# Splitting the results of two attentions, and the first weights of their output projections, inside the attentions on GpSimd

## The chip, the cores and the metric

The kernel runs on one core of a Trainium2 chip. The metric is the device time of one execution in microseconds (us), as the median of several runs. The engines are TensorE (PE, and PEld for its weight loads), VectorE (DVE), ScalarE (ACT), GpSimd (POOL) and SyncE (SP, which issues the DMAs here).

## What is computed

The reference is three transformer layers on 512 latent tokens and 256 context tokens of width 1024. The first layer (a state-space mixer and a convolutional MLP) is not touched. The change lies behind the mixers of the second and third layer:

```python
# layer 2: y = [mlstm_out(ha, oa) (512 wide), window attention (512 wide)] @ w_out, for latent and context tokens
def mlstm_out(h, oa):
    h = rms_norm(h.transpose(0, 2, 1, 3), a_norm_g.reshape(A_HEADS, A_HEAD_DIM))
    return (h.reshape(...) * jax.nn.sigmoid(oa)).astype(oa.dtype)
ob_l = banded_window_attention(qb_l, kb_l, vb_l, kb_c, vb_c, sink)   # 8 heads of 64; context tokens: gqa_attend
y_lat = jnp.concatenate([mlstm_out(ha_l, oa_l), ob_l], axis=-1) @ w_out
# layer 3: y = attention(8 heads of 128, 512 queries on 768 keys) @ w_out, for latent tokens alone
y_lat = gqa_attend(q_blocks, k_all, v_all) @ w_out
# both: x = x + gate * y, and then the MLP
```

## The kernel before

Activations are kept transposed, as tiles of 128 features by tokens: `xT` (the residual stream) and `hT` are eight tiles of 768 tokens (512 latent, 256 context). Weights come as slabs of 1024 by 256 through a ring of four slots (`ring`), which SP fills.

A product of fp32 accuracy is made of three fp32r products. Each operand is split into a high part (rounded to fp32r, `_hi`) and a low part (the operand minus its high part, `_lo`), and PE multiplies hi by hi, hi by lo and lo by hi. The slab is split in two halves, m = 0 and 1, of 128 columns: ScalarE writes `w_hi` (L1232, 128x1024), GpSimd writes `w_lo` (L1237).

The program is a chain of blocks (`nc.Block`), with all engines meeting at a block's end. The blocks that matter here:

- `band_attention` (layer 2): 24 pairs p = (two heads, query block of 128 tokens), six query blocks for each of four pairs of heads. Blocks 0 to 3 are latent and 4 and 5 context, and the keys are 256 to 640 wide. For each pair PE makes the scores (L2714), DVE adds the mask and takes the maximum (`top`, L2773), ScalarE the exponential (L2811), DVE divides each of the two heads by its sum (`norm`, L2785, a TENSOR_SCALAR from SBUF to SBUF), PE transposes (L2726), ScalarE and DVE copy the transposes to SBUF (L2819 and L2793), PE multiplies by the values (L2740) and ScalarE copies the result to `hT` (`give`, L2825). PE runs the scores two pairs ahead. DVE's order is top(p+1), norm(p), the copy of p-1. GpSimd builds the masks, multiplies four tiles of `hT` by the gates (`side`, L2695, 128x768 each), and then has nothing to do.
- `attention` (layer 3): 32 jobs j = (head, block of 128 queries), all 768 keys wide, with the same steps: scores L2540, maximum L2584 (reads PSUM), exponential L2620, `norm` L2602 (TENSOR_SCALAR 128x768), transposes L2551, copy L2628 on ScalarE, values L2562, `give` L2635. GpSimd has no work in it.
- `output_projection`, once behind each (`ab_out` over 768 tokens, `c_out` over 512). It runs `split_stage` with `Halves` as what comes first: ScalarE makes the first slab's two high parts, GpSimd and DVE one low part each, then ScalarE writes the high parts of all of `hT` tile by tile (L662) and DVE the low parts (L667). PE follows tile by tile. For this first slab PE takes the two halves of the weights in turn at each tile, so that both halves are in use until the slab's end:

```python
def unit_order(n_r, first):
    return [(m, r) for r in range(n_r) for m in range(2)] if first else [(m, r) for m in range(2) for r in range(n_r)]
```

In the later slabs PE finishes half 0 before it takes half 1. The high and low part of a half of the next slab are written over those of the same half of the slab before, so ScalarE waits until PE is through with that half.

## Time and profile before

| | before |
|---|---|
| median of 3 runs | 2615.78 us (2614.35 to 2617.09) |
| the profiled execution, its time | 2614.36 us |
| the profiled execution, its span | 2612.6 us |
| mean granted TensorE clock | 0.954 |
| PE busy | 2381.1 us, 91% |
| PEld busy | 1929.9 us, 74% |
| DVE busy | 1231.2 us, 47% |
| ACT busy | 805.5 us, 31% |
| POOL busy | 1003.8 us, 38% |

The time is 1.8 us more than the span, which goes from the first to the last instruction. A share is busy time over the whole span. PE is the busiest by far, but it does not work through: inside an attention each engine waits for another, and between blocks PE waits for what it is to multiply. The second layer's attention lies at 1148 to 1266 us of the span and the third's at about 2068 to 2172 us.

### The profile page before, as it was taken

To read this page: it belongs to the slowest core of one execution; us is meant where nothing else is said; L and a number is where in the kernel's file an instruction comes from. 1 tells how busy PE (TensorE), PEld (TensorE's weight loads), DVE (VectorE), ACT (ScalarE), POOL (GpSimd) and SP (SyncE) were. 2 spreads that over 40 slices of the span, in tenths; PEclk is the share of its full clock that TensorE was granted. 3 is DMA by queue.
4 is the path that set the end of the run, shared out by engine and by line. 5 is a ranking of instruction groups with operands and counts; after the bars stand their busy time and mean duration, and the time that the engine had idled before them with its cause. 6 is when DMAs were issued, how large, how long until landed. Compare 5 with 4: busy or idle time off the path is not lost. (4 is left out here: it accounts for less than half of the span.)

```text
span 2612.6 us, 34942 instructions
## 1 busy us (share of the span) xinstructions
PE 2381.1 (91%) x14323; PEld 1929.9 (74%) x14323; DVE 1231.2 (47%) x1956; ACT 805.5 (31%) x1325; POOL 1003.8 (38%) x606
## 2 busy tenths in 40 slices
PE   6987688999997989967789999999989998899998
PEld 5866466777775779855668888888867687688887
DVE  4417627756555660567436242332427752423432
ACT  4232334333335412335332111111134363322221
POOL 3326234655553322320136343443434002555553
PEclk8998898999997999979899999999989999899999
DMA  8570213444441111100113233333311101233221
GB/s 266 161 226 1 75 49 113 157 153 154 149 145 58 40 48 59 33 1 1 33 49 97 81 113 114 114 127 100 113 41 65 33 1 49 65 97 97 96 97 49
DMA packets 224700, 229.94 MB, mean 88 GB/s; under 512 B 7375, under 2 KB 221219, under 8 KB 224547
## 3 DMA queue, kind: packets, MB, share of 16 engines
q1 hardware_dynamic: 224211, 227.66, 27.1%
q8 instruction: 113, 1.85, 0.3%
q14 instruction: 40, 0.33, 0.0%
q10 hardware_dynamic: 336, 0.11, 0.0%
HBM read 225.65 MB, written 2.10 MB: 87 GB/s over the span
## 5 line engine op out<-in xcount | busy, mean ns | idle before, releaser
L1237 POOL TENSOR_TENSOR w_lo<-ring,w_hi 128x1024 fp32r<-128x1024 f32 x128 | 311.5, 2434 | 431.5 <-ACT w_hi L1232 431.5
L1232 ACT ACTIVATE w_hi<-ring 128x1024 fp32r<-128x1024 f32 x128 | 135.6, 1059 | 738.4 <-PE ps L1297 701.9
L2039 DVE SCALAR_TENSOR_TENSOR xT<-ps,mods,xT 128x512 f32<-128x512 f32 (+1 forms) x160 | 108.3, 683 | 533.0 <-PE ps L1297 474.0
L1295 PE MATMUL ps<-hidden_hi,w_hi 128*128 128x512 f32 (+1 forms) x768 | 273.9, 357 | 5.4 <-POOL hidden_lo L2393 5.4
L1296 PE MATMUL ps<-hidden_lo,w_hi 128*128 128x512 f32 (+1 forms) x768 | 272.1, 354 | 0.0
L1297 PE MATMUL ps<-hidden_hi,w_lo 128*128 128x512 f32 (+1 forms) x768 | 271.6, 354 | 0.0
L2316 DVE SCALAR_TENSOR_TENSOR ffn_sums<-ps,cols,ffn_sums 128x441 f32<-128x441 f32 (+2 forms) x352 | 215.0, 687 | 105.5 <-ACT ffn_sums L2237 105.5
L1295 PE MATMUL ps<-h_hi,w_hi 128*128 128x512 f32 (+1 forms) x720 | 256.4, 356 | 6.7 <-POOL w_lo L1237 3.0
L1296 PE MATMUL ps<-h_lo,w_hi 128*128 128x512 f32 (+1 forms) x720 | 255.0, 354 | 0.0
L1297 PE MATMUL ps<-h_hi,w_lo 128*128 128x512 f32 (+1 forms) x720 | 254.6, 354 | 0.0
L2383 DVE TENSOR_TENSOR squares<-squares 128x512 f32<-128x512 f32 (+1 forms) x72 | 144.9, 2013 | 217.7 <-ACT squares L2369 217.7
L2260 POOL TENSOR_TENSOR ffn_w_lo<-ring,ffn_w_hi 128x1024 fp32r<-128x1024 f32 (+2 forms) x76 | 162.3, 2137 | 184.9 <-ACT ffn_w_hi L2213 184.9
L904 PE MATMUL ps<-h_hi,w_halves 128*128 128x512 f32 (+1 forms) x560 | 205.3, 367 | 17.6 <-POOL c_lo L629 8.6
L1295 PEld LDWEIGHTS ps<-hidden_hi,w_hi 128*128 128x128 f32 x768 | 145.2, 189 | 32.2 <-POOL hidden_lo L2393 8.0
L883 POOL TENSOR_TENSOR ring_low<-ring,w_halves 128x1024 fp32r<-128x1024 f32 x34 | 83.9, 2477 | 211.8 <-ACT w_halves L877 211.8
L1297 PEld LDWEIGHTS ps<-hidden_hi,w_lo 128*128 128x128 f32 x768 | 145.1, 189 | 20.2
L1296 PEld LDWEIGHTS ps<-hidden_lo,w_hi 128*128 128x128 f32 x768 | 145.3, 189 | 19.7
L1295 PEld LDWEIGHTS ps<-h_hi,w_hi 128*128 128x128 f32 x720 | 136.1, 189 | 31.5 <-POOL w_lo L1237 6.1
L2213 ACT ACTIVATE ffn_w_hi<-ring 128x1024 fp32r<-128x1024 f32 (+2 forms) x76 | 71.8, 947 | 255.0 <-PE ps L2202 246.1
L1296 PEld LDWEIGHTS ps<-h_lo,w_hi 128*128 128x128 f32 x720 | 136.2, 189 | 18.8
L1297 PEld LDWEIGHTS ps<-h_hi,w_lo 128*128 128x128 f32 x720 | 136.1, 189 | 18.9
L904 PEld LDWEIGHTS ps<-h_hi,w_halves 128*128 128x128 f32 x560 | 107.4, 192 | 39.5 <-issue 20.5
(448 smaller groups left out, 5223.7 us busy)
## 6 DMA issues: line engine op xcount, KB each, us to landing
ring<-in_mlp_w SPq DMA_DIRECT2D x64, 1024.0 KB, 5.3
ring<-in_ada_w SPq DMA_DIRECT2D x48, 1024.0 KB, 5.3
ring<-in_w_ada SPq DMA_DIRECT2D x24, 1024.0 KB, 9.6
ring<-in_ffn_w_up SPq DMA_DIRECT2D x22, 1024.0 KB, 7.0
ring<-in_ab_w_in SPq DMA_DIRECT2D x11, 1024.0 KB, 5.2
ring<-in_ffn_w_down SPq DMA_DIRECT2D x12, 768.0 KB, 6.0
ring<-in_w_in SPq DMA_DIRECT2D x8, 1024.0 KB, 7.5
ring<-in_c_w_in SPq DMA_DIRECT2D x6, 1024.0 KB, 5.0
```

The lines of the kernel that those rows point to most:

```text
L883: pool.tensor_tensor(low_half(h), ring_half(h), w_halves[:, h % 3, :, :].bitcast(F32), ALU.subtract)\
L904: ins = pe.matmul(o, stationary, moving, start=(k == 0 and i == 0), stop=(k == KT - 1 and i == 2))
L1232: act.activation(w_hi[m][:, 0:x["kt"], :], ring[:, x["n"] % NS, 0:x["kt"], m * P:(m + 1) * P], ACT.Copy).then_inc(SW["w_hi"].sem, 1)
L1237: pool.tensor_tensor(w_lo[m][:, 0:x["kt"], :], ring[:, x["n"] % NS, 0:x["kt"], m * P:(m + 1) * P], w_hi[m][:, 0:x["kt"], :].bitcast(F32), ...
L1295: pe.matmul(o, w_hi[m][:, k, :], h, start=(k == 0), stop=False)
L1296: pe.matmul(o, w_hi[m][:, k, :], l, start=False, stop=False)
L1297: ins = pe.matmul(o, w_lo[m][:, k, :], h, start=False, stop=(k == x["kt"] - 1))
L2039: return nc.vector.scalar_tensor_tensor(x, bank, column_of(gates, t * 2 + 2 * gate + r), x, ALU.mult, ALU.add)
L2213: act.activation(w_hi[i % NW][:, 0:kt, :], ring[:, n % NS, 0:kt, m * P:(m + 1) * P], ACT.Copy).then_inc(SW["w_hi"].sem, 1)
L2260: pool.tensor_tensor(w_lo[i % NW][:, 0:kt, :], ring[:, n % NS, 0:kt, m * P:(m + 1) * P], w_hi[i % NW][:, 0:kt, :].bitcast(F32), ALU.subtract)\
L2316: ins = dve.scalar_tensor_tensor(o, on_grid(ps[:, (first + m) % 4, :])[:, y0 + dy:y1 + dy, x0 + dx:x1 + dx], cols[:, CW + tap * 2 * FT + t ...
L2383: dve.tensor_tensor(sq, sq, sq, ALU.mult).then_inc(v_order.sem, 1)
```

## The change

Inside `band_attention` GpSimd now splits each result of the attention as `give` has written it, 128 tokens of one tile at a time: a CAST to the high part and a TENSOR_TENSOR for the low part. The low part is written over `hT` itself. The four gated tiles are split whole (128x768) behind their multiplications, one at each of the first four pairs. In the middle of the attention ScalarE writes the two high parts of the first output slab, and GpSimd the two low parts. `attention` gets the same, with no gated tiles. The projection (`made_projection`) starts with its products at once, and its first slab is taken like the others, half 0 and then half 1.

```diff
+        class Made:
+            low_on_dve, made = False, True
...
+            def weights_high(self, act):
+                wait_slab(act, self.n)
+                for m in range(2):
+                    act.activation(self.w_hi[m][:, :, :], ring[:, self.n % NS, :, m * P:(m + 1) * P], ACT.Copy)\
+                       .then_inc(SW["w_hi"].sem, 1)
+
+            def weights_low(self, pool):
+                for m in range(2):
+                    pool.wait_ge(SW["w_hi"].sem, SW["w_hi"].at(m + 1))
+                    pool.tensor_tensor(self.w_lo[m][:, :, :], ring[:, self.n % NS, :, m * P:(m + 1) * P],
+                                       self.w_hi[m][:, :, :].bitcast(F32), ALU.subtract).then_inc(SW["w_lo"].sem, 1)
+
+            def split(self, pool, k, t0, n):
+                x, hi = hT[:, k, t0:t0 + n], self.hi[:, k, t0:t0 + n]
+                g_order.step(pool, pool.tensor_copy(hi, x))
+                pool.tensor_tensor(self.lo[:, k, t0:t0 + n], x, hi.bitcast(F32), ALU.subtract)
...
-                    x["first"] = prev_w is None
+                    x["first"] = prev_w is None and not norm.made
...
 @@ attention, GpSimd @@
-                    for dst, factor in side:
-                        pool.tensor_tensor(dst, dst, factor, ALU.mult)
+                    for j in range(n_jobs):
+                        h, n = divmod(j, NLAT)
+                        wait(pool, "pv_out", j + 1)
+                        made.split(pool, h, n * CH, CH)
+                        if j == n_jobs - 6:
+                            made.weights_low(pool)
...
 @@ attention, ScalarE, behind give(j - 1) @@
+                        if j == n_jobs - 7:
+                            made.weights_high(act)
...
 @@ band_attention, GpSimd @@
+                    def gated_side(pool, i):
+                        dst, factor = side[i]
+                        g_order.step(pool, pool.tensor_tensor(dst, dst, factor, ALU.mult))
+                        made.split(pool, i, 0, TOK)
+
+                    def out_split(pool, p):
+                        hp, n = pairs[p]
+                        wait(pool, "pv_out", p + 1)
+                        made.split(pool, 4 + hp, n * CH, CH)
...
-                    for dst, factor in side:
-                        pool.tensor_tensor(dst, dst, factor, ALU.mult)
+                    for p in range(n_p):
+                        if p < len(side):
+                            gated_side(pool, p)
+                        out_split(pool, p)
+                        if p == n_p // 2:
+                            made.weights_low(pool)
...
 @@ band_attention, ScalarE, behind give(p - 1) @@
+                        if p == n_p // 2:
+                            made.weights_high(act)
```

The masks of the band attention move to the buffer `squares`, and `va` and `ka` change places in memory, so that the high parts fit over `qa` and `va`. The numbers of instructions for the masks stay as they were.

GpSimd's instructions at the start of the band attention, before. `big` holds the masks, and the four TENSOR_TENSOR are the gates.

```order
190 L2691 MEMSET big 128x896
191 L2692 COPY big<-mats 128x128 [waits g_order]
192 L2693 COPY big<-mats 128x128
193 L2695 TENSOR_TENSOR hT<-hT,big 128x768 x4
194 L2688 UNCONDITIONAL_BRANCH
195 L1338 UNCONDITIONAL_BRANCH [waits barrier_Pool_Activation_PE_DVE_SP_gather]
196 L1237 TENSOR_TENSOR ab_out_w_lo<-ring,ab_out_w_hi 128x1024 [waits w_hi] x7
```

The same place after the change. `h_hi_7351` is the low part, a second name for `hT`'s memory, and `pv_out` is the signal of `give`.

```order
190 L2750 MEMSET squares 128x896
191 L2751 COPY squares<-mats 128x128 [waits g_order]
192 L2752 COPY squares<-mats 128x128
193 L2742 TENSOR_TENSOR hT<-hT,big 128x768
194 L666 CAST ab_out_hi<-hT 128x768 [waits g_order]
195 L667 TENSOR_TENSOR h_hi_7351<-hT,ab_out_hi 128x768 [waits g_order]
196 L666 CAST ab_out_hi<-hT 128x128 [waits pv_out]
197 L667 TENSOR_TENSOR h_hi_7351<-hT,ab_out_hi 128x128 [waits g_order]
198 L2742 TENSOR_TENSOR hT<-hT,big 128x768
```

The gates are now spread over four pairs, each followed by two more instructions of the same size, and each pair of the attention has a CAST and a TENSOR_TENSOR of its own.

ScalarE's instructions in the middle of the band attention, after the change (L2874 is the exponential, L2882 the copy of the transposes, L2888 `give`). Before, the same rows stood there without the two of L655.

```order
528 L2882 ACTIVATE big<-ps 128x512 [waits pv,turned]
529 L2888 ACTIVATE hT<-ps 128x128 [waits pv]
530 L655 ACTIVATE ab_out_w_10639<-ring 128x1024 [waits slot_loaded1]
531 L655 ACTIVATE ab_out_w_10640<-ring 128x1024
532 L2874 ACTIVATE big,small<-big,small 128x641 [waits top] x2
```

The two conversions of weights stand ahead of the exponentials of pair 14.

GpSimd's instructions near the end of the last attention, after the change (before, it had none in this block).

```order
445 L667 TENSOR_TENSOR h_hi_16911<-hT,c_out_hi 128x128 [waits g_order]
446 L661 TENSOR_TENSOR c_out_w_18004<-ring,c_out_w_18002 128x1024 [waits w_hi]
447 L661 TENSOR_TENSOR c_out_w_18005<-ring,c_out_w_18003 128x1024 [waits w_hi]
448 L666 CAST c_out_hi<-hT 128x128 [waits pv_out]
449 L667 TENSOR_TENSOR h_hi_16911<-hT,c_out_hi 128x128 [waits g_order]
```

The two low parts of the weights stand between the splits of jobs 26 and 27.

## Rows read from the trace of the kernel before

**Rows 1.** timeline, end of the band attention to the first product of `ab_out`

```profile
1265.54 0.28 ACT L2825 ACTIVATE hT<-ps 128x128 f32<-128x128 f32 x1 [0.84 <-PE ps L2740]
1266.10 2.00 ACT L1232 ACTIVATE ab_out_w_hi<-ring 128x1024 fp32r<-128x1024 f32 x2 [0.28 <-PEq L2688]
1267.23 2.39 POOL L1237 TENSOR_TENSOR ab_out_w_lo<-ring,ab_out_w_hi 128x1024 fp32r<-128x1024 f32 x1 [110.06 <-ACT ab_out_w_hi L1232]
...
1271.45 0.77 PE L1276 MATMUL ps<-ab_out_h_hi,ab_out_w_hi 128*128 128x512 f32 x1 [5.95 <-DVE ab_out_h_lo L667]
```

**Rows 2.** timeline, end of the last attention and first product of `c_out`

```profile
2171.39 0.28 ACT L2635 ACTIVATE hT<-ps 128x128 f32<-128x128 f32 x1 [1.06 <-PE ps L2562]
...
2177.27 0.77 PE L1276 MATMUL ps<-c_out_h_hi,c_out_w_hi 128*128 128x512 f32 x1 [5.91 <-DVE c_out_h_lo L667]
```

**Rows 3.** timeline, PE's first product of the second weight slab, `ab_out` and `c_out`

```profile
1293.04 0.50 PE L1295 MATMUL ps<-ab_out_h_hi,ab_out_w_hi 128*128 128x512 f32 x1 [3.27 <-POOL ab_out_w_lo L1237]
...
2193.82 0.50 PE L1295 MATMUL ps<-c_out_h_hi,c_out_w_hi 128*128 128x512 f32 x1 [2.96 <-POOL c_out_w_lo L1237]
```

**Rows 4.** windows: stretch, its us, busy us of each engine, TensorE clock, DMA, GB/s

```profile
1186.90:1192.20 5.30, 3.86 (x24) 1.87 (x24) 3.20 (x11) 2.62 (x7) 0.00 (x0) 1.00 0.01 2
1237.60:1245.60 8.00, 6.15 (x24) 3.10 (x24) 4.08 (x14) 2.66 (x6) 0.00 (x0) 0.67 0.00 1
1271.40:1274.50 3.10, 3.05 (x7) 2.48 (x8) 3.10 (x6) 3.10 (x10) 0.00 (x0) 0.50 0.81 253
1289.80:1293.00 3.20, 0.00 (x0) 0.00 (x0) 0.53 (x2) 1.71 (x2) 2.36 (x2) 1.00 0.00 0
2177.20:2182.40 5.20, 5.13 (x12) 4.10 (x13) 4.14 (x7) 0.92 (x2) 0.00 (x0) 0.50 0.64 202
```

**Rows 5.** timeline, VectorE and GpSimd at the same moments in the MLP

```profile
1389.59 2.66 DVE L2383 TENSOR_TENSOR rstd<-rstd 128x256 f32<-128x256 f32 x1
...
1389.48 2.50 POOL L1237 TENSOR_TENSOR w_lo<-ring,w_hi 128x1024 fp32r<-128x1024 f32 x1
```

**Rows 6.** timeline, VectorE and GpSimd as the band attention opens

```profile
1150.08 7.10 POOL L2695 TENSOR_TENSOR hT<-hT,big 128x768 f32<-128x768 f32 x4
1150.15 1.75 DVE L2758 TENSOR_SCALAR small<-rows 128x8 f32<-128x8 f32 x1 [1.75 <-POOL big L2693]
...
1152.01 0.74 DVE L2773 CUSTOM_DVE_ANT_0 big<-ps,big,small 128x512 f32<-128x512 f32 x1
```

**Rows 7.** groups of instructions by form, GpSimd: count, busy us, mean ns, idle before

```profile
L2695 POOL TENSOR_TENSOR hT<-hT,big 128x768 f32<-128x768 f32 x4 | 7.1, 1809 | 0.0
...
L1031 POOL TENSOR_TENSOR narrow_parts<-wnarrow,narrow_parts 128x128 fp32r<-128x128 f32 x2 | 0.9, 450 | 0.0
...
L2693 POOL COPY big<-mats 128x128 f32<-128x128 f32 x1 | 0.3, 296 | 0.0
```

**Rows 8.** timeline, one pair of heads and block, ScalarE and VectorE

```profile
1251.85 0.28 ACT L2825 ACTIVATE hT<-ps 128x128 f32<-128x128 f32 x1 [1.36 <-PE ps L2740]
...
1252.47 0.56 DVE L2785 TENSOR_SCALAR big<-big,small 128x640 f32<-128x640 f32 x1
...
1253.13 0.56 DVE L2785 TENSOR_SCALAR big<-big,small 128x640 f32<-128x640 f32 x1
...
1255.45 0.49 DVE L2773 CUSTOM_DVE_ANT_0 big<-ps,big,small 128x256 f32<-128x256 f32 x1 [1.03 <-PE ps L2726]
```

**Rows 9.** timeline, a pair at block 0, ScalarE and VectorE

```profile
1212.24 0.28 ACT L2825 ACTIVATE hT<-ps 128x128 f32<-128x128 f32 x1 [0.43 <-PE ps L2740]
...
1213.66 0.49 DVE L2785 TENSOR_SCALAR big<-big,small 128x512 f32<-128x512 f32 x1
```

**Rows 10.** timeline, one job of the last attention, ScalarE and VectorE

```profile
2113.14 0.28 ACT L2635 ACTIVATE hT<-ps 128x128 f32<-128x128 f32 x1 [0.53 <-PE ps L2562]
2113.31 0.90 ACT L2620 ACTIVATE big<-ps,small 128x768 f32<-128x768 f32 x1
...
2115.68 0.62 DVE L2602 TENSOR_SCALAR big<-big,small 128x768 f32<-128x768 f32 x1
```

More of the change, by code:

```diff
@@ L1252, in _ @@
                 def _(pe):
-                    norm.pe(pe)
+                    if not made:
+                        norm.pe(pe)
                     def body(s, seg, i):
@@ L1340, in _ @@
                     x = next(x for x in segs[0]["items"] if "n" in x)
-                    for m in range(1 if norm.low_on_dve else 2):
-                        low(pool, x, None, segs[0], m)
-                    norm.pool(pool)
+                    if not made:
+                        for m in range(1 if norm.low_on_dve else 2):
+                            low(pool, x, None, segs[0], m)
+                        norm.pool(pool)
                     if "pool_start" in after_of:
@@ L1362, in _ @@
                 def _(dve):
-                    if norm.low_on_dve:
+                    if norm.low_on_dve and not made:
                         low(dve, next(x for x in segs[0]["items"] if "n" in x), None, segs[0], 1)
-                    norm.dve(dve)
+                    if not made:
+                        norm.dve(dve)
                     def body(s, seg, i):
@@ L1381, in split_stage @@
                 t.close(kinds[k])
-            norm.close()
+            if not made:
+                norm.close()
         n_small, dve_abs = [0], [0, 0]
@@ L2050, in post_norm, with made_projection @@
                         lambda k, r: cols[:, COL[b] + k:COL[b] + k + 1], sems=FIRST_NORM)
+        def made_projection(name, ranges, made):
+            gated, items = add_gated(16), []
+            for j in range(4):
+                items.append(("w", W[name] + j, KT, (made.hi, made.lo, 0), ranges, "dve",
+                              lambda i, m, r, bank, un, j=j: gated(2 * j + m, r, bank), {}))
+            split_stage((made.w_hi, made.w_lo), [(items, 1)], made)
+            stage.close()
         def output_projection(name, ranges, more=None, second_ctx=False):
@@ L2513, in rope, with attention @@
                 R[n].close(len(tiles))
-        def attention(jobs, scale, bufs, side=()):
+        def attention(jobs, scale, bufs, made):
             sc, pt, stat = bufs
```

43 lines of the change are left out of this document (27 added, 16 removed).

## The prediction

> **What bounds the kernel now.** I read the timeline around the two places where an attention hands over to its output projection, because the change moves work from there. The reader is to see in it how long PE stands still. The band attention's last `give` starts at 1265.54 and takes 0.28, so its result is there at 1265.82. Then ScalarE and GpSimd make the first weights, and PE's first product starts at 1271.45, 5.95 us idle [rows 1]. The last attention's `give` ends at 2171.67, and PE starts at 2177.27, 5.91 us idle [rows 2]. A second wait follows one slab later: 3.27 us in `ab_out` and 2.96 us in `c_out`, both for GpSimd's `w_lo` [rows 3]. It comes from the first slab's order, in which both halves of the weights are in use until the end. Then I read windows for the TensorE clock. It is at its lower level, 1.2 GHz (0.50), for the first 3.1 us of `ab_out` and the first 5.2 us of `c_out`, and after the wait of 3.2 us at 1289.80, in which it stayed at 1.00, nothing is lost [rows 4].
>
> Against these gains stands what GpSimd's new instructions do to VectorE, which I read where the two run together. In the MLP a TENSOR_TENSOR 128x256 of VectorE starts at 1389.59 and takes 2.66 us: it ends at 1392.25, just behind GpSimd's 128x1024 that ends at 1391.98 [rows 5]. At the head of the band attention a TENSOR_SCALAR of eight columns takes 1.75 us, and ends with the first of GpSimd's four gates (7.10 / 4 = 1.78 us each), not with the fourth. The `top` that follows at 1152.01 runs 0.74 us while the gates still go on [rows 6]. So a VectorE instruction of these kinds is held until the GpSimd instruction in progress ends and gets its turn there; `top`, which reads PSUM, is not held. `norm` is a TENSOR_SCALAR from SBUF to SBUF, the kind that is held.
>
> **The change, part by part.** Gains:
>
> 1. *The wait at each hand-over.* After the last `give` GpSimd has one CAST and one TENSOR_TENSOR of 128x128. The nearest rows are a COPY 128x128 of 0.30 us and a TENSOR_TENSOR 128x128 of 0.45 [rows 7]. With two semaphores (0.07 us each; GpSimd's wait at 1267.23 follows ScalarE's first w_hi, half of 2.00 us from 1266.10) that is 0.89, and the end of the block adds the 0.28 that lies between 1265.82 and 1266.10 [rows 1], and 0.2 for the first weight load. PE starts 1.37 us behind the last `give`: at 1267.2 instead of 1271.45, and at 2173.05 instead of 2177.27. 4.25 + 4.2 = **8.4 us**.
> 2. *The second wait.* With half 0 finished first, its successor is made beside half 1, as in the later slabs. 3.27 + 2.96 = **6.2 us**.
> 3. *The clock.* PE's idle time falls from 5.9 us to about 1.6, and the wait of 3.2 us did not lower the clock [rows 4]. I take it that the projections start at 2.4 GHz, which returns half of 3.1 and of 5.2 us: **4.2 us**. The other end is 0.
>
> Costs. In both attentions the chain of a pair runs through VectorE. In [rows 8] the norms stand at 1252.47 and 1253.13, and `top` can start at 1255.45 only when PE has transposed what they wrote; VectorE's other time there is busy. What holds `norm` holds the chain.
>
> 4. *Small splits in the band attention.* Counted from a `give`'s start, GpSimd's CAST lies at 0.35 to 0.64 and its TENSOR_TENSOR at 0.71 to 1.16. Where the norms stand at +0.62 and +1.28 [rows 8], the first is not held (0.02), the TENSOR_TENSOR waits for it, and the second is held until about 1.63: 0.36 us. At block 0 the norm stands at +1.42 [rows 9], behind both: nothing. The six positions of a group come out at 0.36, 0.19, 0, 0.40, 0 and 0, so about 0.95 for six pairs, and for the 20 pairs behind the gates **2.8 us**. From below the bound is 0. From above it is both instructions for every pair, 0.75 x 20 = 15.
> 5. *The gated tiles.* Three of the four lie beside norms (the first ends before pair 0's). Each is TENSOR_TENSOR 1.81, CAST, TENSOR_TENSOR 1.81 [rows 7]. No row has a CAST of 768 on GpSimd; between 0.30 (the small COPY) and 1.81 I take 1.1, nearer to the middle since a copy reads one operand. That is 4.8 us each. For the six norms of pairs 2 to 4, walked through with GpSimd back to back, I get holds of 0.7, 1.7, 0, 1.0, 1.6 and 1.0: **6.0 us**. The bounds are 3 (half of it falls on waits for PE) and 9 (each norm held for half to all of 1.8).
> 6. *The weights' low parts.* Two instructions of about 2.5 us [rows 5] back to back. In the band attention one norm meets the second of them from its start: **2.4**. In the last attention the norm stands at +2.54 and the first instruction at about 1.24 to 3.7: **1.2**. Together 3.6, between 0 and 9.9 (all four in full).
> 7. *The weights' high parts.* 2.0 us on ScalarE behind a `give` [rows 1]. In the band attention at pair 12, block 0's long wait for scores covers it: 0, and without that cover up to 2. In the last attention the exponential starts at once behind `give` at 2113.31, takes 0.90 plus its accumulator, and norm follows at +2.54, so some 1.1 us of the 2.0 is slack [rows 10]: **1.0**.
> 8. *Small splits in the last attention.* `give` at 2113.14, norm at 2115.68, the split done at +1.16 [rows 10], and the norm before lies ahead of `give`: **0**, in all 32 jobs. If the cover of 1.4 us went, it would be 0.3 each.
>
> The high and low parts that leave the hand-over (L662, L667 and the first w_hi and w_lo) are already in items 1 and 2. DMAs are not moved past anything: SP's next slab is issued in the projection's block as before, some 4 us earlier.
>
> Sum: gains 8.4 + 6.2 + 4.2 = 18.8; costs 2.8 + 6.0 + 3.6 + 1.0 = 13.4; net **5.4 us less**. Against the profiled execution's 2614.36 that gives 2609.0. It lay 1.4 under the median of the runs shown, so against the median 2615.78 I say **2610.4 us**. By layer, the second gains 4.25 + 3.27 + 1.6 and pays 11.2, and so ends 2 us slower; the third gains 4.2 + 2.96 + 2.6 and pays 2.2, and so is 7.5 us faster.
>
> On item 4 the Trainium skill, "SBUF — State Buffer", section "Who interferes with whom", says that VectorE and GpSimd contend for one shared pair of ports as an exclusive lock, and that whoever issues first keeps it for the whole instruction. By that rule, the trace agrees for VectorE's side (the 2.66 us); no row here shows a GpSimd instruction waiting behind a TENSOR_SCALAR, as my walk assumes. By the rule the sum is the one above; without that part, with GpSimd going on beside a norm, the first hold of a pair in item 4 would be shorter and the second longer.
>
> **The rivals.**
>
> - *The holds reach every pair* (slower). Place: `norm` in the band attention. If GpSimd's two small instructions hold it in full in all 20 pairs, item 4 costs 15 instead of 2.8, and the time is 2610.4 + 12.2 = 2622.6. The point from which the change loses is (2.8 + 5.4) / 20 = 0.41 us of hold for each pair; for over 0.2% it is 0.67. For it: norm and split do meet in [rows 8]. Against it: block 0's distance in [rows 9], and that each delay moves the two apart.
>   The Trainium skill's "Perfetto Trace Analysis", section "Optimizing Scalar/DVE Operations", says that moving operations between GpSimd and VectorE might not help for this reason. By it the time would be at this rival's end.
> - *The holds do not reach the end.* If VectorE's waits for PE (1.03 us in [rows 8]) take up items 4 to 6, only item 7 is left: 18.8 - 1.0, so 2598. For it: VectorE idles in every pair. Against it: that idle time itself follows from the norms.
> - *The clock does not come back, and falls in one more place.* The stretch 1237.60 to 1245.60 took 8.00 us at a mean clock of 0.67, where the twin group's 1186.90 to 1192.20 took 5.30 at 1.00 [rows 4]. Stretched pairs leave PE idler, so another such place can come (2.7 us), and item 3 can fail (4.2): 2617.3. It can also go the other way, if the low stretch at 1237 disappears.
> - *The change does not shorten the hand-over*, since GpSimd runs late at the end. Its 0.8 us per pair stands against 1.1 us between the last two `give`s (0.84 idle and 0.28, [rows 1]), so I give this 3 in 100; with items 1 and 3 gone it would be 2623.
>
> **How the numbers follow.** A measurement of this kernel tells 0.2%, 5.2 us, from no change, so the forecast lies on that edge. Chances: forecast (net 1 to 10 us less) 0.52; holds in every pair 0.13; holds absorbed 0.13; clock 0.19; no shorter hand-over 0.03. Half of the forecast's case lies beyond 5.2 us, and with the absorbed case and a small part of the clock case (it can gain too) faster has 0.26 + 0.13 + 0.05 = 0.44. Same has the other 0.26, 0.12 of the clock case, and 0.05 of the holds and the last case together: 0.43. Slower has the rest, 0.13, nearly all of it holds. The bounds of items 3, 5 and 6 alone carry the forecast from 2604 to 2617; with the parts of the rivals that lie next to it the range is 2602 to 2619.
>
> **What would show it.** Right: PE's idle time at the two hand-overs is 1.2 to 2 us, and no PE wait over 1 us for `w_lo` in either projection; the first products at 0.23 us apart. `norm` in the last attention keeps 0.62 us but for one or two of 32; in the band attention the norms of pairs 2 to 4 take 1 to 2 us, some others 0.6 to 0.9. The band attention is 11 us longer and the last one 2. Wrong: a CAST 128x768 of 2 us or more; `top` held too, which would double the costs; norms of the last attention held in each job; or a clock of 0.50 at the first products.

## The result, and the profile after

| | before | after |
|---|---|---|
| median | 2617.28 us (8 runs, 2611.97 to 2621.53) | 2605.24 us (8 runs, 2599.0 to 2608.97) |
| ratio | | 0.9949, 95% interval 0.9938 to 0.9960 |
| the profiled execution, its span | 2612.6 us | 2601.9 us |

The change makes the kernel 0.51% faster: 12.0 us by the medians, 13 by the ratio. The forecast was 5.4 us less. The result lies inside the range of the prediction and on the side that it held likeliest by a hair (faster 0.44, same 0.43), and the gain is somewhat over twice the forecast.

The page of the profiled execution after the change, its totals:

```profile
span 2601.9 us, 35012 instructions
PE 2377.1 (91%) x14323; PEld 1927.4 (74%) x14323; DVE 1222.1 (47%) x1930; ACT 794.8 (31%) x1301; POOL 1065.0 (41%) x728
```

GpSimd is busy 61 us more than before, and PE as long as before to 4 us. So what changed is when PE works, not how much it has to do. The timeline at the end of the band attention, to be held against [rows 1]:

```profile
1273.31 0.28 ACT L2888 ACTIVATE hT<-ps 128x128 f32<-128x128 f32 x1 [0.84 <-PE ps L2803]
1273.65 0.29 POOL L666 CAST ab_out_hi<-hT 128x128 fp32r<-128x128 f32 x1 [0.29 <-ACT hT L2888]
1274.02 0.45 POOL L667 TENSOR_TENSOR h_hi<-hT,ab_out_hi 128x128 fp32r<-128x128 f32 x1
...
1274.81 0.47 PE L1325 MATMUL ps<-ab_out_hi,ab_out_w 128*128 128x512 f32 x1 [1.53 <-PEq L2737]
```

The last `give` is now followed by one small split alone, and PE starts 1.50 us behind the start of the `give`, 1.22 behind its end, after 1.53 us of idle time where it had been 5.95. The end of the last attention, against [rows 2], shows the same 1.53:

```profile
2171.21 0.28 ACT L2682 ACTIVATE hT<-ps 128x128 f32<-128x128 f32 x1 [1.06 <-PE ps L2609]
...
2172.71 0.47 PE L1325 MATMUL ps<-c_out_hi,c_out_w 128*128 128x512 f32 x1 [1.53 <-PEq L2569]
```

Windows over the first 5.3 us of both projections (busy time and count of each engine, then PEclk, the granted clock):

```profile
1274.80:1280.10 5.30, 5.29 (x23) 4.39 (x24) 0.00 (x0) 0.00 (x0) 0.00 (x0) 1.00 0.64 201
2172.70:2178.00 5.30, 5.29 (x23) 4.41 (x24) 0.00 (x0) 0.00 (x0) 0.00 (x0) 1.00 0.61 198
```

The clock is at 1.00 (2.4 GHz) from the first product, where [rows 4] had 0.50. Twenty-three matmuls run in 5.3 us.

Now the price, inside the band attention. The gated tiles of pairs 2 and 3, from the timeline:

```profile
1179.55 0.83 POOL L666 CAST ab_out_hi<-hT 128x768 fp32r<-128x768 f32 x1
1180.46 1.81 POOL L667 TENSOR_TENSOR h_hi<-hT,ab_out_hi 128x768 fp32r<-128x768 f32 x1
1180.59 1.96 DVE L2848 TENSOR_SCALAR big<-big,small 128x512 f32<-128x512 f32 x1
...
1182.66 0.49 DVE L2848 TENSOR_SCALAR big<-big,small 128x512 f32<-128x512 f32 x1
...
1185.81 0.46 DVE L2848 TENSOR_SCALAR big<-big,small 128x256 f32<-128x256 f32 x1
1186.20 1.81 POOL L667 TENSOR_TENSOR h_hi<-hT,ab_out_hi 128x768 fp32r<-128x768 f32 x1
1186.37 1.78 DVE L2848 TENSOR_SCALAR big<-big,small 128x256 f32<-128x256 f32 x1
```

A `norm` that starts 0.13 or 0.17 us behind GpSimd's long TENSOR_TENSOR takes 1.96 and 1.78 us, 1.4 to 1.5 more than the same `norm` takes before. But each gated tile hits one norm in this way, and the other norm of the pair goes through in 0.49 or 0.46 (0.56 at the last gated tile). A pair with a small split:

```profile
1206.60 0.28 ACT L2888 ACTIVATE hT<-ps 128x128 f32<-128x128 f32 x1 [1.36 <-PE ps L2803]
1206.94 0.29 POOL L666 CAST ab_out_hi<-hT 128x128 fp32r<-128x128 f32 x1 [3.90 <-ACT hT L2888]
1207.22 0.56 DVE L2848 TENSOR_SCALAR big<-big,small 128x640 f32<-128x640 f32 x1
1207.32 0.78 POOL L667 TENSOR_TENSOR h_hi<-hT,ab_out_hi 128x128 fp32r<-128x128 f32 x1
1207.88 0.56 DVE L2848 TENSOR_SCALAR big<-big,small 128x640 f32<-128x640 f32 x1
```

Here GpSimd is the one that waits: its TENSOR_TENSOR starts 0.10 us behind `norm` and takes 0.78 us instead of 0.45. The second `norm` is not held at all. All 48 norms together, in the groups of instructions by line:

```profile
L2848 DVE TENSOR_SCALAR big<-big,small 128x512 f32<-128x512 f32 (+2 forms) x48 | 29.5, 614 | 1.7
L2649 DVE TENSOR_SCALAR big<-big,small 128x768 f32<-128x768 f32 x32 | 20.8, 649 | 1.1
```

The same two groups in the kernel before:

```profile
L2785 DVE TENSOR_SCALAR big<-big,small 128x512 f32<-128x512 f32 (+2 forms) x48 | 22.3, 465 | 1.7
L2602 DVE TENSOR_SCALAR big<-big,small 128x768 f32<-128x768 f32 x32 | 19.8, 620 | 1.1
```

Norms cost 7.2 us more in the band attention and 1.0 more in the last one. Taken norm by norm against before, the 7.2 are 4.6 in five norms at the gated tiles, 1.6 in one norm beside a low part of the weights (1236.70, 2.08 us), and 0.9 in six norms beside small splits. The one beside the low part, with the two `give`s around it:

```profile
1233.54 4.96 POOL L661 TENSOR_TENSOR ab_out_w<-ring,ab_out_w 128x1024 fp32r<-128x1024 f32 x2
...
1236.70 2.08 DVE L2848 TENSOR_SCALAR big<-big,small 128x512 f32<-128x512 f32 x1
1236.83 0.28 ACT L2888 ACTIVATE hT<-ps 128x128 f32<-128x128 f32 x1 [2.01 <-PE ps L2803]
...
1242.17 0.28 ACT L2888 ACTIVATE hT<-ps 128x128 f32<-128x128 f32 x1 [2.04 <-PE ps L2803]
```

In the last attention the two low parts lie beside two norms as forecast. The rows of the timeline are:

```profile
2160.10 5.05 POOL L661 TENSOR_TENSOR c_out_w<-ring,c_out_w 128x1024 fp32r<-128x1024 f32 x2
2161.52 1.39 DVE L2649 TENSOR_SCALAR big<-big,small 128x768 f32<-128x768 f32 x1
2162.26 0.28 ACT L2682 ACTIVATE hT<-ps 128x128 f32<-128x128 f32 x1 [0.53 <-PE ps L2609]
...
2164.81 0.76 DVE L2649 TENSOR_SCALAR big<-big,small 128x768 f32<-128x768 f32 x1
...
2165.55 0.28 ACT L2682 ACTIVATE hT<-ps 128x128 f32<-128x128 f32 x1 [0.53 <-PE ps L2609]
```

The norms are held by 0.77 and 0.14 us, and the two `give`s still lie 3.29 us apart. That is the step of before too, in 28 of its 31 (the last three are shorter, since PE has no scores left to make). PE is what ends each job here (107.72 us busy of 108.70 in the window 2062.5 to 2171.2), and `norm` has slack.

### The profile page after: what moved, and what is told of

The parts are those of the page before. It is cut to its first block and busy times, and to the rows that moved or that the text cites. A ratio compares the mean times of both kernels' runs of the same rounds, so it can differ in the third digit from the quotient of the medians.

```text
span 2601.9 us, 35012 instructions
## 1 busy us (share of the span) xinstructions
PE 2377.1 (91%) x14323; PEld 1927.4 (74%) x14323; DVE 1222.1 (47%) x1930; ACT 794.8 (31%) x1301; POOL 1065.0 (41%) x728
```

## The stretches, one execution beside another

The profiled pair does not explain itself alone: the block of the band attention begins at 1148.68 us before and at 1152.88 after, though nothing ahead of it was changed. So I measured the same stretches in every kernel that was run, each in its one profiled execution, by the starts of the same instructions: A from the first memset of the band attention to its last `give`; then PE's idle time before the first product; P from the first product to the first sums of the MLP's normalization; and the same for the last attention (from its first scores, which in before are at 2062.85 us, somewhat ahead of the 2068 given above). "low" is the time in A at 1.2 GHz, worked out as twice one minus the granted clock, times A.

| kernel | block begins | A | low in A | idle | P of `ab_out` | last attention | idle | P of `c_out` |
|---|---|---|---|---|---|---|---|---|
| before | 1148.68 | 116.86 | 34 | 5.95 | 75.86 | 108.54 | 5.91 | 53.72 |
| before_2 | 1151.01 | 120.86 | 44 | 5.92 | 75.81 | 108.51 | 5.94 | 53.72 |
| before_3 | 1153.89 | 117.68 | 38 | 5.93 | 75.95 | 108.64 | 5.92 | 53.61 |
| c_only | 1150.03 | 117.71 | 38 | 5.91 | 78.54 | 109.45 | 1.53 | 48.02 |
| after | 1152.88 | 120.42 | 27 | 1.53 | 70.93 | 108.76 | 1.53 | 48.01 |
| again | 1150.97 | 128.53 | 55 | 1.53 | 72.53 | 108.69 | 1.53 | 48.00 |
| band_only | 1154.37 | 125.11 | 44 | 1.54 | 72.52 | 108.51 | 5.94 | 53.74 |
| by_turns | 1151.51 | 122.75 | 34 | 1.68 | 77.30 | 108.78 | 1.68 | 52.93 |
| late | 1152.54 | 125.31 | 41 | 6.43 | 73.47 | 109.45 | 6.43 | 50.86 |
| weights_late | 1150.65 | 119.72 | 31 | 5.04 | 73.50 | 108.44 | 5.05 | 50.97 |
| doubled | 1151.73 | 125.14 | 41 | 3.46 | 73.28 | 110.33 | 3.35 | 48.01 |
| aligned | 1155.34 | 119.59 | 31 | 1.53 | 70.92 | 108.77 | 1.53 | 48.01 |
| head | 1153.80 | 116.21 | 24 | 1.53 | 70.94 | 108.68 | 1.53 | 48.01 |
| head_w | 1149.81 | 120.53 | 41 | 1.53 | 72.55 | 108.76 | 1.53 | 48.01 |

Before the change A has 116.86, 120.86, 117.68 and 117.71 us (c_only has its code too), mean 118.3. With the changed code (after, again, band_only, by_turns, late) it has 120.42 to 128.53, mean 124.4. The scatter within one code is the clock's: the longest A, that of again, has the most time at the low clock. With a scatter of 4 and 8 us the two means alone would leave the difference of 6.1 uncertain by some 3 us.

The steps from the start of one `give` to the next tell it more sharply, since wherever the clock stays at 1.00 they repeat within 0.02 us from one execution to another. Five of them, in us:

| from the `give` of pair | before | after | head | beside it in after |
|---|---|---|---|---|
| 1 to 2 | 3.74 | 6.06 | 3.75 | a gated tile |
| 2 to 3 | 2.91 | 3.60 | 3.00 | a gated tile |
| 3 to 4 | 3.56 | 4.69 | 3.57 | a gated tile |
| 8 to 9 | 2.91 | 3.00 | 3.01 | small splits alone |
| 13 to 14 | 3.74 | 5.34 | 5.35 | a low part of the weights |

A low stretch of the clock, 3.4 us long, lies in the first two steps of after; the other steps shown ran at 1.00. So the gated tiles cost 4.1 us on the path, with what this low stretch costs in it. The low part of the weights costs 1.60, as much as its norm is held (1.59); in weights_late and head_w, which don't have it there, the step is 3.75 and 3.74. The small splits cost 0.09 in six pairs, 0.3 in those behind the gated tiles. Together that is 6.0, the same as by the means.

## The experiments

All are the changed kernel with one edit, unless said otherwise. Ratios are to the kernel before, with 95% intervals.

**The two layers apart (c_only, band_only).**

```diff
 c_only: in the band attention and behind it
-                    for p in range(n_p):
-                        if p < len(side):
-                            gated_side(pool, p)
-                        out_split(pool, p)
...
+                    for dst, factor in side:
+                        pool.tensor_tensor(dst, dst, factor, ALU.mult)
...
-        made_projection("ab_out", BOTH, ab_made)
+        output_projection("ab_out", BOTH)
 band_only: the like in the last attention and behind it
-        made_projection("c_out", ONLY_LAT, c_made)
+        output_projection("c_out", ONLY_LAT)
```

> The change in layer 3 alone: the band attention and ab_out are as before, the last attention and c_out as after. By the two traces layer 3 gains 9.9 us (hand-over and projection 10.1 less, attention 0.2 more): about 2607.4 against a before of 2617.3, ratio 0.9962. By the prediction's terms it gains 7.5: 2609.8, ratio 0.9971. A rival, that half of the 12 us measured came from stages that the change doesn't touch (by the shifted memory, which this kernel has too), expects the sum of this kernel's and the next one's gain to be clearly under 12.

> The change in layer 2 alone: the last attention and c_out are as before. By the two traces it gains 5.8 us (band attention 3.6 more, hand-over and projection 9.4 less): ratio 0.9978. By the prediction's terms it loses 2: ratio 1.0008. These two lie 8 us apart, so the ratio's sign decides.

Measured: c_only 0.9966 (0.9952 to 0.9979), so 8.9 us less; band_only 0.9994 (0.9981 to 1.0007), so 1.6 us less, give or take 3.4. The sum, 10.5, agrees with the 12 of both, but its own uncertainty of 5 us would just admit the 6 of the rival, that half of the gain comes from elsewhere. It falls by the stretches, which put more than 6 into layer 3 alone. Layer 3 is settled: attention, idle time and projection take 168.2 us in all four executions with the old code and 158.2 to 159.0 in the six with the new (c_only, after, again, aligned, head, head_w): 9.9 less, 9.2 in c_only itself, whose last attention began in a low stretch of 6.8 us where after's began in one of 3.4. Layer 2's sign is not: neither the 5.8 us less of the first pair of traces nor the 2 us more of the prediction is inside the interval (5.0 less to 1.8 more), and its first pair of traces had flattered the change.

**Once more (again, before_2, before_3).** The kernels unaltered.

> The changed kernel once more, unaltered, for the scatter from one profiled execution to the next. Both theories: ratio 0.995. Band attention 120 us from its first memset to its last give and 3 to 5 us longer than before's; if the stretch from 772 to 1148 us, which came out 3.5 longer in the first pair of traces, is only scatter, it comes out otherwise here; if it belongs to the kernel (memory layout), it is 3.5 longer again.

> The kernel before once more, unaltered, for the scatter of its stretches. In its first profile the band attention took 116.86 us and the projection behind it 75.86; where its code stood unchanged in another kernel they took 117.71 and 78.54, with more time at 1.2 GHz. Theory (the clock alone makes the scatter): attention 116 to 119 here, projection 75.9 to 78.6, last attention 108.5, c_out 53.7. The rival (scatter as wide as after's, 120 to 128.5) expects up to 125 in the attention.

> The kernel before once more, as the run ahead of this one and with its expectations: band attention 116 to 119 us and projection 75.9 to 78.6 if the clock alone scatters them, up to 125 in the attention by the rival.

Measured: again 0.9952 (0.9936 to 0.9968); the two of before have one time each, 2623.95 and 2620.72 us. The 3.5 us ahead of the band attention are scatter: the block begins anywhere between 1148.68 and 1155.34. My "120 us, 3 to 5 longer" for the attention was wrong, since again took 128.53. The windows over the band attention, first after:

```profile
1152.90:1273.30 120.40, 88.05 (x704) 57.64 (x704) 81.41 (x233) 55.81 (x146) 43.51 (x63) 0.89 0.00 1
```

and again:

```profile
1151.00:1279.50 128.50, 98.92 (x704) 65.00 (x704) 81.43 (x233) 55.64 (x146) 43.60 (x63) 0.79 0.00 1
```

VectorE (third), ScalarE and GpSimd are busy equally long to 0.2 us, so the holds are the same in every execution. PE's 704 matmuls take 10.9 us longer, and the clock is 0.79 instead of 0.89. The same window of before_2, with VectorE at 74.23, 7.2 less:

```profile
1151.00:1271.90 120.90, 95.42 (x704) 61.75 (x704) 74.23 (x233) 53.81 (x145) 8.44 (x7) 0.82 0.00 1
```

So before's attention scatters by 4 us too: 120.86 lies outside the 116 to 119 that was expected of before_2, and a part of its rival holds. The Trainium skill, "TensorE: Matmul & The Clock Gate", section "Part 1: The HAM clock gate", says of the start of a kernel that the same kernel shows a different count of matmuls at the low clock from run to run. These rows agree in the middle of a kernel too, and put its worth at 8 us in 120.

**The first slab's order (by_turns).**

```diff
-                    x["first"] = prev_w is None and not norm.made
+                    x["first"] = prev_w is None
```

> As after, but PE takes the two halves of the first slab in turn at each tile, as before, in both projections. By item 2 of the prediction a wait of 3.3 and 3.0 us for the second slab's low part comes back: 6.2 us more than after, ratio to before 0.9973. A rival: the wait of item 2 came from the weights of the second slab starting late with the block, not from the order, and then this kernel is as after.

Two more lines of the edit only leave out steps that belong to the making of `hT`'s parts. Measured: 1.001 (1.0001 to 1.0019), 0.6% more than after, 14 us by the medians and 16 by the ratios where 6.2 were expected. With this order the gain of the whole change is gone. Of the 14 to 16, 11.3 lie in the two projections (below) when held against after's profiled execution; the rest is within the intervals, some 4 us. PE's timeline at the start of the second slab, in `c_out`:

```profile
2191.92 0.39 PE L1309 MATMUL ps<-c_out_hi,c_out_w 128*128 128x512 f32 x1
2192.86 4.78 POOL L1266 TENSOR_TENSOR c_out_w<-ring,c_out_w 128x1024 fp32r<-128x1024 f32 x2 [12.16 <-ACT c_out_w L1261]
...
2195.32 0.50 PE L1326 MATMUL ps<-c_out_hi,c_out_w 128*128 128x512 f32 x1 [3.02 <-POOL c_out_w L1266]
```

The wait itself is what item 2 says, 3.28 us in `ab_out` and 3.02 here. What item 2 leaves out comes behind it, in the windows of this kernel:

```profile
1275.90:1293.00 17.10, 16.88 (x96) 14.80 (x96) 1.97 (x4) 0.48 (x1) 0.00 (x0) 1.00 0.20 62
1295.30:1302.10 6.80, 6.04 (x14) 4.83 (x15) 0.00 (x0) 0.00 (x0) 3.08 (x2) 0.50 0.36 119
2196.50:2199.90 3.40, 3.40 (x10) 2.63 (x9) 0.00 (x0) 0.00 (x0) 1.13 (x1) 0.50 0.26 54
```

PE had worked through the first slab at 1.00, and after the wait it has 6.8 and 3.4 us at 0.50. P grows by 6.4 and 4.9 us (77.30 against 70.93, 52.93 against 48.01), 11.3 in all: 6.3 of wait and 5.0 of clock. The kernel before can pay this too: in c_only, whose `ab_out` has the old code, the clock falls behind the same wait, and P takes 78.54 instead of the 75.8 to 76.0 of the three others. [Rows 4] had shown me one that didn't fall. That was the common case, though: of the eight such waits in the executions of the old code, four in `ab_out` and four in `c_out`, the clock stayed at 1.00 through seven, and c_only's is the one that fell. PE was at 1.00 ahead of all ten, so why it fell in both projections of by_turns and in one of eight otherwise is not shown.

```profile
1293.90:1300.70 6.80, 5.36 (x13) 4.20 (x14) 0.00 (x0) 0.00 (x0) 3.75 (x2) 0.50 0.26 80
```

**The weights inside the attentions (weights_late).**

```diff
 in both attentions
-                            made.weights_high(act)
-                            made.weights_low(pool)
 in the projection's block, ScalarE and GpSimd
+                    if made:
+                        high(act, x, None, segs[0], 0)
+                        high(act, x, None, segs[0], 1)
...
+                        low(pool, x, None, segs[0], 0)
+                        low(pool, x, None, segs[0], 1)
```

> As after, but the first slab's high and low parts are made at the start of the projection's block (ScalarE 2 x 1.0, GpSimd 2 x 2.4) and no longer inside the attentions. PE then starts about 3.4 us later at each hand-over (1.0 + 2.4 + a semaphore): 6.8 us more in the two, plus what the clock loses (0 to 4). What it gets back is the price of the weights inside the attentions: 4.6 us by the prediction (2.4 band, 1.2 and 1.0 last attention), at most 1 by the traces. So ratio to after +2 us by the prediction, +6 or more by the traces.

Measured: 0.9987 (0.9978 to 0.9996), 8 to 10 us more than after, on the traces' side and not on the prediction's. PE's idle time is 5.04 and 5.05 us, 3.5 more each, and `c_out` starts at 0.50, which costs 2.96 us there (50.97 against 48.01), and 1.0 to 2.6 in `ab_out`. What comes back inside the attentions is small: the norms' excess in the band attention is 5.5 us instead of 7.2, so the weights' low parts cost 1.6 there, and in the last attention the first and the last `give` lie 97.71 us apart instead of 97.83, so there they cost 0.12, high parts included.

**Twice the small splits (doubled).**

```diff
             def split(self, pool, k, t0, n):
                 x, hi = hT[:, k, t0:t0 + n], self.hi[:, k, t0:t0 + n]
+                if n == CH:
+                    g_order.step(pool, pool.tensor_copy(hi, x))
+                    spare = squares.rearrange("p a n -> p (a n)")[:, 1024:1024 + CH]
+                    g_order.step(pool, pool.tensor_tensor(spare, x, hi.bitcast(F32), ALU.subtract))
```

> As after, but every small split (128x128) has a second CAST and a second TENSOR_TENSOR (to a spare tile): 1.5 us of GpSimd per pair where there were 0.75. If VectorE's norm is on the path in the band attention as the prediction has it, 20 pairs pay another 0.2 to 0.45 each: 4 to 9 us more there. If PE's or another engine's slack takes it up, under 2. In the last attention the prediction says 0 for one split of 0.75 that ends 1.4 us ahead of norm; the doubled one ends at about 1.9 behind give where norm stands at 2.5, so 0 again; a rival, that GpSimd's small ones disturb every job, gives 32 x 0.1 or more = over 3 us. Plus at each hand-over 0.75 more of the last split: 1.5 in all.

Measured: 0.9999 (0.9988 to 1.0009), some 12 us more than after. VectorE's norms take 30.1 us instead of 29.5 in the band attention, 0.6 us more in all, of which 0.2 lie beside small splits (1.1 instead of 0.9) and 0.4 beside the weights' low parts. At 1.00 the steps between `give`s with small splits alone are as in after (2.91 us before, 3.00 here), so twice the small work costs nothing more there; A, at 125.14, lies within the scatter of the unaltered code. In the last attention the jobs stay 3.29 us apart but for one of 3.64 beside the weights' high parts, made up by the next of 3.06, and one of 3.84 beside their low parts. There `norm` takes 2.27 us, held by 1.65, and PE waits for it: 0.55 of the 1.65 reach the step, so `norm` can be some 1.1 us late before PE waits.

```profile
2170.51 5.04 POOL L661 TENSOR_TENSOR c_out_w<-ring,c_out_w 128x1024 fp32r<-128x1024 f32 x2
...
2171.03 2.27 DVE L2653 TENSOR_SCALAR big<-big,small 128x768 f32<-128x768 f32 x1
...
2173.36 0.88 PE L2602 MATMUL ps<-mats,big 128*128 128x128 f32 x6 [0.34 <-DVE big L2653]
```

What does show is at the end: PE's idle time is 3.46 and 3.35 us, 1.9 and 1.8 more where I had reckoned 0.75. With 1.5 us of GpSimd's time for each result and `give`s 1.1 us apart GpSimd runs late in the last pairs, the mechanism of the fourth rival, which needs twice the work. Against the mean of the unaltered kernels the stretches account for some 7 of the 12 us; the rest I can't place, and the intervals are 4 us wide.

**PE held up for another 4.9 us (late).**

```diff
 behind the last split of both attentions
+                    for _ in range(2):
+                        g_order.step(pool, pool.tensor_tensor(squares.rearrange("p a n -> p (a n)")[:, 0:1024],
+                                                              xT[:, 0:2, 0:LAT], xT[:, 2:4, 0:LAT], ALU.subtract))
```

> As after, but behind the last split GpSimd does two more instructions of 128x1024 (about 2 x 2.4 us, to a spare tile) in each attention's block, so that PE starts some 4.8 us later, with all else as in after. It tells the idle time from the clock: if an idle time of about 6 us brings the clock down at the first products, as before, the cost is 2 x 4.8 plus up to 4.2 (item 3) = 13.8 us; if the clock stays at 1.00, 9.6.

Measured: 1.0032 (1.0021 to 1.0043), about 21 us more than after. The windows of the first products:

```profile
1284.20:1289.50 5.30, 5.26 (x13) 4.12 (x14) 0.00 (x0) 0.00 (x0) 0.00 (x0) 0.50 0.66 198
2191.50:2196.80 5.30, 5.28 (x13) 4.19 (x14) 0.00 (x0) 0.00 (x0) 0.00 (x0) 0.50 0.66 198
```

With 6.43 us of idle time PE makes 13 matmuls in the time of 23, as item 3 says. The idle times cost 9.8 us, and the projections 2.85 (`c_out`) and 0.9 to 2.5 (`ab_out`) more: 13.6 to 15.2, against 13.8 expected. The theory that the clock stays up, 9.6, falls. Another 2.9 us lie in the third layer's MLP (384.1 us from its first sums to the end, against 381.2 in after), where 24 us are at the low clock, against 18 in after.

**GpSimd told to wait for the norms (aligned).**

```diff
                     for p in range(n_p):
...
+                        if p + 1 < n_p:
+                            wait(pool, "norm", 2 * p + 4)
                         made.split(pool, 4 + hp, n * CH, CH)
+                        if p in extra:    # one of: gate, high, low of tile i (p = 3i, 3i+1, 3i+2), low part of the weights (13, 14)
+                            extra[p][0](extra[p][1])
```

> As after, but in the band attention GpSimd waits, before each pair's instructions, until VectorE has finished both norms of the next pair, and its twelve long instructions on the gated tiles and the two low parts of weights come one to a pair, behind the small split. No norm should be held by a long one. If holds of norm are what lengthens the band attention, it gets as long as before: about 3.6 us less than after by the two traces (ratio to before 0.9938), 11.2 less by the prediction's terms. A rival: the holds cost nothing on the path, and the longer band attention is the TensorE clock's doing; then it is as after within 1 us. In all norms of L2848's kind the mean should fall from 0.49 to under 0.40.

Measured: 0.9937 (0.9923 to 0.9952). That is what the two traces had given (0.9938), but the interval takes in after's 0.9949 as well, so it doesn't decide. The edit did not do what it was for. The mean of the norms fell from 614 ns only to 586 (the 0.49 in its expectation was their median and not the mean, and before's own mean is 465, so the 0.40 could not have come), and three norms, of pairs 5, 7 and 11, are still held by 1.4 us each. In those pairs the norms lie too close for 0.75 and 1.81 us behind the wait. So it is no clean test of what the holds cost.

**The gated tiles at the head (head, head_w).** After's trace shows where they fit: GpSimd waits 17.45 us for the first `give`, beside PE at its first scores.

```profile
1157.05 1.81 POOL L667 TENSOR_TENSOR h_hi<-hT,ab_out_hi 128x768 fp32r<-128x768 f32 x1
...
1162.61 4.23 PE L2777 MATMUL ps<-big 64*128 64x512 f32 x8 [1.91 <-DVE small L2836]
...
1176.32 0.29 POOL L666 CAST ab_out_hi<-hT 128x128 fp32r<-128x128 f32 x1 [17.45 <-ACT hT L2888]
```

```diff
 head
+                    for i in range(len(side)):
+                        gated_side(pool, i)
                     for p in range(n_p):
-                        if p < len(side):
-                            gated_side(pool, p)
                         out_split(pool, p)
 head_w: besides
+                    made.weights_low(pool)        # behind the gated tiles
-                        if p == n_p // 2:
+                        if p == 0:
                             made.weights_high(act)
```

> As after, but GpSimd multiplies and splits all four gated tiles at the head of the band attention, ahead of the first pair's small split, and no longer one at each of pairs 0 to 3. After's trace shows it idle there for 17.45 us (1158.86 to 1176.31); the three tiles that move take 4.4 us each, 13.3 in all, and end about 4 us ahead of the first give. The three norms of 1.8 to 2.0 us beside pairs 2 to 4 should be gone (sum of the 48 norms 29.5 us before it, 25 to 26 here); norms of pairs 0 and 1 may be held in their place, where PE is at its scores for another 3 and 1.3 us. If the long holds cost what they take, the band attention is 4 us shorter than after's (mean of five executions 124.4), and if they also start the clock's low stretches at 31 and 45 us from the block's start, 3 to 4 more: ratio to before 0.991 to 0.993. If holds cost nothing, as after: 0.995.

> As the kernel with the gated tiles at the head, and the weights' high parts (ScalarE, behind the copy of pair 0) and low parts (GpSimd, behind the gated tiles) there too. GpSimd then works to about 1177 us, past the first give at 1176, so one or two norms of pairs 1 and 2 meet a low part, and the norm of 2.1 us in the middle goes. If only the number of held norms counts, no change against the kernel before this; if holds late in the attention cost more through the clock, 1 to 3 us less.

Measured: head 0.9937 (0.9924 to 0.9951), head_w 0.9934 (0.9921 to 0.9948). The medians are 2601.49 and 2602.36 us, against 2619.55 for before. Both beat the kernel before, by 16 and 17 us by the ratio; against after (0.9949, 0.9938 to 0.9960) the intervals overlap, so that they beat it too is likely but not settled. The traces say more. A norm held at the head of head:

```profile
1163.52 4.22 PE L2777 MATMUL ps<-big 64*128 64x512 f32 x8 [1.91 <-DVE small L2836]
1163.58 1.02 DVE L2848 TENSOR_SCALAR big<-big,small 128x512 f32<-128x512 f32 x1
...
1164.71 1.83 DVE L2848 TENSOR_SCALAR big<-big,small 128x512 f32<-128x512 f32 x1
...
1167.67 1.97 PE L2789 MATMUL ps<-mats,big 128*128 128x128 f32 x8
```

The two norms of pair 0 are held, end at 1166.54, and the transposes wait for PE's own scores until 1167.67. All norms take 28.4 us, only 1.1 less than in after and not the 25 to 26 expected, yet A is 4.2 us shorter at about the same clock (0.90 and 0.89). The steps above place it: 4.0 us in the three beside after's gated tiles, while the first `give` of head, which comes behind its three held norms (by 0.53 and 1.35 us in pair 0, 1.36 in pair 1), lies 22.9 us into the block, and after's 23.1. So these holds cost nothing where PE is busy. Where PE waits, a hold costs most or all of its length: 1.60 for 1.59 at the weights' low part, and 1.13 for 1.64 in the step from pair 3 to 4. The low stretch of 3.4 us that starts 31 to 32 us into the block, behind the hold at the gated tile, stands in all seven executions with after's order of the gates, and in none of the other seven; that the hold brings it is likely by this, but not shown. head_w shows no more gain than head, as the first of its theories has it; its A of 120.53 has the clock at 0.83. It does save the 1.6 us of the step from pair 13 to 14 (3.74 instead of 5.35), but its low clock hides that in A.

## Why the prediction was right in sign and half in size

The gains of the sum were right, and the costs were put at twice what they are. By the stretches of several executions, the gains are 8.8 (idle times), 6.2 (second waits) and 2.8 to 4.4 (clock), 18 to 19 against 18.8 forecast; the costs are 6.1 (124.4 minus 118.3, and 6.0 by the steps) and 0.2, against 13.4. 18.6 minus 6.3 is 12.3, and the medians say 12.0; that they agree to 0.3 is luck, since each is uncertain by more. By layer, the third gains 8.9 to 9.9 where 7.5 was forecast, and the second 1.6, give or take 3.4, where a loss of 2 was.

1. *The wait at each hand-over*: 8.4 forecast, 8.80 measured. PE starts 1.22 us behind the end of the last `give`, where I had 1.37. Right.
2. *The second wait*: 6.2 forecast. Both waits are gone, and in seven of the eight in the old code they were worth what they took. In the eighth (c_only) and in by_turns the clock went down with the wait, which in by_turns makes it worth 11.3 instead of 6.3. So the size was right for the kernel before, but one window where the clock held was too little to call that loss nothing.
3. *The clock*: 4.2 forecast. `c_out` gains 2.75 in each of its executions (53.72 minus 2.96, against 48.01). `ab_out` gains 1.7 in after, aligned and head, and 0.1 in again, band_only and head_w, where the clock falls for 3.4 us just as the products start. So 2.8 to 4.4. That the idle time of 5 to 6 us is what brought it down is shown by late and weights_late.
4. *Small splits in the band attention*: 2.8 forecast, 0.9 measured on the norms (1.1 for twice as many), and 0.3 to 0.4 on the path. The failed step is the walk's "the second is held until about 1.63". In the trace the second norm takes its 0.56 us though GpSimd's row still shows 0.22 us in progress. Of the 20 pairs, five to seven show a norm held, by 0.10 or 0.25.
5. *The gated tiles*: 6.0 forecast, 4.6 measured. The CAST takes 0.82 us, not 1.1. Five norms are held, three of them by 1.4 to 1.5 and two by 0.1 and 0.2, where the walk had 1.6, 1.7 and three more of 0.7 to 1.0; they are norms of pairs 3 to 5, and not 2 to 4. On the path they cost 4.1, 4.0 when held against head, and both have what the low stretch costs in them.
6. *The weights' low parts*: 3.6 forecast, 1.6 in the band attention (of 2.4), all of it on the path, and nothing that shows on the path in the last (of 1.2). The two norms there are held by 0.77 and 0.14, but the failed step is the one ahead of the list: "in both attentions the chain of a pair runs through VectorE". In the last one it runs through PE, with `norm` some 1.1 us off the path (doubled).
7. *The weights' high parts*: 0 and 1.0 forecast. The job behind them takes 3.64 us and the next 3.06, together 0.12 more than two of 3.29. Same failed step as in item 6: slack on PE takes it back within one job.
8. *Small splits in the last attention*: 0 forecast, 0 measured, even doubled.

The rivals. *Holds reach every pair* falls (item 4). *Holds do not reach the end* is true of the last attention, and of the band attention only where PE is at its scores. *The clock falls in one more place* is half right: it does, 31 to 32 us into the block in every execution that has after's order of the gates, and other executions of the same code show up to 27 us more of low clock than the first. But the old code has such places too. *No shorter hand-over* falls, and doubled shows how far off it is.

One sum of the prediction is off: with item 6 at its upper bound too, the bounds of items 3, 5 and 6 carry the forecast up to 2624 and not to 2617. The result lies towards the other end, so it doesn't hang on this.

On item 4 the Trainium skill, "SBUF — State Buffer", section "Who interferes with whom", has one lock, kept by whoever issues first for the whole instruction. The trace agrees on both sides now: `norm` held for 1.78 us behind a TENSOR_TENSOR that started 0.17 us earlier, and GpSimd's small one held from 0.45 to 0.78 behind a `norm`. The second norm at 1207.88, which is not held, the rule does not give; whether the end of GpSimd's row is late there, no run tells.

What stays open: the size of layer 2's gain, 1.6 us give or take 3.4, since A scatters by 8 us with the clock; what decides whether the clock falls at a wait of 1.5 to 3.5 us; and whether head is faster than after.

## What to carry to other kernels

Work moved to an idle engine costs what it holds up, and only there: find for each held instruction the engine that ends the step (PE in one attention here, VectorE in the other), and place long instructions where that engine is busy anyway, as at the head of a block. A wait of PE between two warm stretches should be priced with the clock behind it, 3 us of wait being worth up to 6.4 here (and no more than itself in seven of ten cases), so an order that keeps PE fed (one half of the weights finished before the other) can be worth as much as the rest of a change. And a stretch whose clock scatters has to be read from several executions of the same code, or from steps that ran at the same clock, before a difference of a few us is explained.

## What the runs showed of the hardware

- After 1.5 to 1.7 us of idle time the clock was at 1.00 at the first product in all of seven `c_out`, and fell to 0.50 for 3.4 us within 0.5 us of the start in three of seven `ab_out`. After 3.35 us it held once and after 3.46 us it did not; after 5.0 us and more it was at 0.50 at the first product in all cases. At the waits of 2.96 to 3.28 us for the second slab, with PE at 1.00 ahead of them, it fell in three of ten.
- The same code of a band attention took 120.42 to 128.53 us, with 27 to 55 us at 1.2 GHz, and VectorE's busy time equal to 0.2 us.
- GpSimd's CAST to fp32r takes 0.82 us for 128x768 and 0.29 for 128x128; its TENSOR_TENSOR 1.81 and 0.45.
- VectorE's `norm` of 0.49 and 0.35 us took 1.96 and 1.78 us when a TENSOR_TENSOR of GpSimd (1.81 us) had started 0.13 and 0.17 us ahead of it, and GpSimd's of 0.45 us took 0.78 when it started 0.10 us behind a `norm`.
